# First filter products beside the last projections, and half of an output tile under the last inverse transforms

## The reference, cut to what matters

```python
parts = jnp.split(dwconv_centred(hy, hy_conv_w, hy_conv_b), 1 + HY_ORDER, axis=-1)
filters = hyena_filters(L, hy_w1, hy_b1, hy_w2, hy_b2, hy_w3, hy_freq)
u = parts[0]
for o in range(HY_ORDER):
    u = parts[o + 1] * long_conv(u, filters[:, o], hy_bias[o])
return jnp.concatenate([y, u], axis=-1) @ w_out, final

def long_conv(u, h, bias):          # y = irfft(rfft(u) * rfft(h)) + u * bias
```

## Time and profile before

| | before |
|---|---|
| median of 3 runs | 1463.18 us (1462.31 to 1465.86) |
| the profiled execution, own time | 1463.94 us |
| its span (first to last instruction) | 1462.1 us |
| TensorE busy | 1230.1 us, 84% of the span |
| last Hyena projection ends | 422.5 us |
| spectrum of turn 0 ends, turn 1's tokens begin | 448.8 us |
| turns 1 and 2, each | 26.9 us |
| output projection begins | 549.6 us |
| first expert slot free | 672.75 us |

### The profile page before, as it was taken

The page is one execution under the profiler, slowest core; times in us unless marked ns, Lnnn a source line. Parts: engine busy times, 40 slices in busy tenths (PEclk is TensorE's granted clock), DMA queues, the critical chain, the costliest instruction groups (busy, mean ns, idle before and its releaser), DMA issues.

```text
span 1462.1 us, 16614 instructions
## 1 busy us (share of the span) xinstructions
PE 1230.1 (84%) x6357; PEld 694.8 (48%) x6357; DVE 458.2 (31%) x950; ACT 338.1 (23%) x850; POOL 197.0 (13%) x267
## 2 busy tenths in 40 slices
PE   3899889899989989977997774699888959987771
PEld 1465454555445554455554442453455446544430
DVE  0104467533227860051111111321364341110104
ACT  3212276210022300041111111313253221111103
POOL 1000012100022301001211111125001011111101
PEclk9999999999999999988999998699999979999996
DMA  9985400276930125246999995933312559999993
GB/s 329 366 305 183 173 29 1 96 264 253 340 109 0 58 115 197 115 173 247 378 418 420 419 418 226 347 70 42 130 59 88 182 177 378 417 419 420 420 374 139
DMA packets 94494, 339.77 MB, mean 232 GB/s; under 512 B 12768, under 2 KB 16550, under 8 KB 69729
## 3 DMA queue, kind: packets, MB, share of 16 engines
q1 hardware_dynamic: 71296, 296.89, 52.0%
q0 software_dynamic: 16240, 35.08, 8.0%
q10 hardware_dynamic: 6897, 6.97, 1.4%
HBM read 336.69 MB, written 23.18 MB: 246 GB/s over the span
## 4 chain that ended last, share of the span: by engine, by line
PE 57%; DMA 18%; DVE 6%; ACT 3%; issue 2%; POOL 1%; ACTq 0%; DVEq 0%; POOLq 0%; SPq 0%
PE bank L780 52%; DMA ring<-in_moe_w_down_dram 17%; PE bank L784 4%; PE bank L811 1%; DMA arena<-expert_rows 1%; DVE arena L2247 1%; DVE arena L2249 1%; ACT ring L1768 0%; DMA hT<-rows,scr 0%; DVE xR L2251 0%; DMA expert_rows<-arena,scr 0%; POOL arena L2397 0%; ACT hT L1444 0%; ACT rstd L1418 0%; DVE arena L2269 0%
## 5 line engine op out<-in xcount | busy, mean ns | idle before, releaser
L780 PE MATMUL bank<-ring,arena 128*64 128x256 f32 (+4 forms) x2976 | 482.6, 434 | 64.4 <-DMA ring<-in_moe_w_down_dram 23.5
L780 PEld LDWEIGHTS bank<-ring,arena 128*64 128x64 f32 (+1 forms) x2976 | 247.2, 145 | 261.7 <-issue 147.2
L780 PE MATMUL bank<-hT,ring 128*128 128x384 f32 (+2 forms) x904 | 304.5, 498 | 6.4 <-ACT hT L1444 6.4
L780 PEld LDWEIGHTS bank<-hT,ring 128*128 128x128 f32 (+1 forms) x904 | 174.0, 194 | 134.6 <-issue 16.6
L2222 DVE TENSOR_TENSOR hT<-hT,bank 128x256 f32<-128x256 f32 x32 | 13.5, 421 | 279.4 <-ACT hT L1656 279.4
L780 PE MATMUL bank<-arena 128*64 128x32 bf16 (+9 forms) x560 | 76.5, 356 | 12.8 <-DVE arena L2195 4.5
L784 PE MATMUL bank<-cst,arena 128*128 128x128 f32 (+3 forms) x207 | 36.2, 335 | 60.7 <-ACT arena L1431 37.3
L780 PE MATMUL bank<-arena,ring 128*128 128x256 f32 (+3 forms) x272 | 63.1, 385 | 12.1 <-DVE ring L2083 7.0
L1656 ACT ACTIVATE hT<-bank 128x256 f32<-128x256 f32 x32 | 12.3, 384 | 260.9 <-PE bank L780 260.9
L784 PE MATMUL bank<-cst,hT 128*128 128x128 f32 x368 | 61.1, 301 | 12.2 <-DMA hT<-rows,scr 12.2
L784 PEld LDWEIGHTS bank<-cst,hT 128*128 128x128 f32 x368 | 47.4, 190 | 48.9 <-issue 35.9
(11 more groups left out here) (287 smaller groups left out, 1152.4 us busy)
## 6 DMA issues: line engine op xcount, KB each, us to landing
ring<-in_moe_w_gate_dram SPq DMA_DIRECT2D x30, 2048.0 KB, 19.6
ring<-in_moe_w_up_dram SPq DMA_DIRECT2D x30, 2048.0 KB, 21.5
ring<-in_moe_w_down_dram SPq DMA_DIRECT2D x30, 2048.0 KB, 22.4
ring<-in_w_ada_dram SPq DMA_DIRECT2D x24, 2048.0 KB, 14.7
ring<-in_ev_w_in_dram SPq DMA_DIRECT2D x11, 2048.0 KB, 11.5
ring<-in_ev_w_out_dram SPq DMA_DIRECT2D x4, 2048.0 KB, 15.1
arena<-expert_rows POOLq DMA_DIRECT2D x6, 1024.0 KB, 7.0
ring<-in_od_w_in_dram SPq DMA_DIRECT2D x3, 2048.0 KB, 21.0
```

The lines of the kernel that those rows point to most:

```text
L780: return nc.tensor.matmul(out, lhsT, rhs, start=start, stop=stop_, skip_group_check=True)
```

## The change

1. Turn 0's six filter products are issued right behind projection ("hy", 2, 5), with their copies on ScalarE and multiplications on GpSimd; they go to storage of their own (`pq0`, in `scr`, `rstdw` and the arena from 14336, where `gstage` lies), so ScalarE waits first until the gates are stored. `hs` is made on VectorE behind ("hy", 2, 3). The loads "hypar1" move to the slot of block ("ada", 1, 10) and so come right behind "hypar0"; the scratch slot becomes that of ("hy", 2, 1).
2. Turn 0's mirror product is issued behind the two H products.
3. The output projection's chunks 0 to 7 of token tile 0 (16 products) are issued in the last turn between spectrum and prompt inverse. The other tiles' chunks 0 to 7 follow the sample inverse without waiting for the gating; only from block 2 on is the gating waited for. The projection's banks are renumbered (`OUT_BANK`), also for the jobs behind it. `wout` 3 is loaded as soon as the last prompt inverse is done, behind one expert block in SP's list.

```diff
-HY_SLOTS = [k % NSLOT for k in (len(FIRST) - 6, len(FIRST) - 5)]
-HY_LENT = (len(FIRST) - 1) % NSLOT
+HY_PARAMS = [len(FIRST) - 6, len(FIRST) - 7]
+HY_SLOTS = [k % NSLOT for k in HY_PARAMS]
+HY_LENT = (len(FIRST) - 5) % NSLOT
+OUT_BANK = (6, 0, 1, 4, 5, 2, 3, 7)
+FILTERS_AFTER = ("hy", 2, 5)
...
         def own(*banks):
-            return banks if l == 0 else (None, None)
+            return tuple(OUT_BANK[b] for b in banks) if l == 0 else (None, None)
...
+        pq0 = ([scr[:, 0:512], rstdw[:, :]], area(14336, 2, 2, 512))
...
                 if k == len(FIRST) - 1:
-                    sp.wait_ge(done, JOB[LAST_INV] + 1)
+                    sp.wait_ge(done, JOB[LAST_SPEC_S] + 1)
...
+            def first_states():
+                pe.wait_ge(S("yn"), KD)
+                arrived(("wout", 0))
+                arrived(("wout", 1))
+                for h in range(2):
+                    took(pe, *PLAN[PRIOR[JOB[("wout", 0, h)]]][0])
+                    for k in range(KD):
+                        product(0, h, k)
+
+            def filters(turn, b, o):
+                for i, (s, x, t) in enumerate(HY_FILTERS):
+                    ps = open_bank("PQ", b, o, s, x, t)
+                    mm(ps[:, :], (hsP, hsQ)[x][:, cols(s + t)], w3s[:, b, o, :], True, True).then_inc(done, 1)
+                    if i == 0 and turn:
+                        mirror(b, o)
...
+                    if ("hy", q, c) == FILTERS_AFTER:
+                        pe.wait_ge(S("hs"), 1)
+                        pe.wait_ge(S("hypar0_in"), 16 * 6)
+                        filters(0, *HYO[0])
...
-            pe.wait_ge(S("hs"), 1)
             pe.wait_ge(S("hconv"), 3 * KD)
-            pe.wait_ge(S("hypar0_in"), 16 * 6)
...
-            filters(*HYO[0])
+            tokens(*HYO[0])
             prompt_response(0, *HYO[0])
+            mirror(*HYO[0])
             sample_response(0, *HYO[0])
             for turn, (b, o) in enumerate(HYO):
                 more = turn + 1 < len(HYO)
                 spectrum(b, o)
                 if more:
-                    filters(*HYO[turn + 1])
+                    tokens(*HYO[turn + 1])
+                    filters(turn + 1, *HYO[turn + 1])
+                else:
+                    first_states()
                 prompt_back(turn, b, o)
...
-            took(pe, *LAST_INV)
-            pe.wait_ge(S("yn"), KD)
...
                 for b in range(3):
                     arrived(("wout", b))
-                    for t in range(NT):
+                    if b == 2:
+                        took(pe, *LAST_INV)
+                    for t in range(1 if b < 2 else 0, NT):
...
+                if ("hy", c // KD, c % KD) == FILTERS_AFTER:
+                    act.wait_ge(S("gates_out"), 16 * 2)
+                    take_filters(0, *HYO[0])
...
-            for which, (block, b) in enumerate(((LOADS[len(FIRST) - 6], 0), (LOADS[len(FIRST) - 5], 1))):
+            for which, (block, b) in enumerate(((LOADS[HY_PARAMS[0]], 0), (LOADS[HY_PARAMS[1]], 1))):
```

More of the change, by code:

```diff
@@ L168, in bank_plan, with tokens, filters @@
                 job(("gr", 1), "act")
-    def filters(b, o):
+    def tokens(b, o):
         for t, bank in ((0, 6), (2, 7), (1, 6)):
             job(("utk", b, o, t), "act", None, bank)
+    def filters(b, o):
         for i, (s, x, t) in enumerate(HY_FILTERS):
             job(("PQ", b, o, s, x, t), "act", None, (7, 6, 1)[i % 3])
-            if i == 0:
+            if i == 0 and (b, o) != HYO[0]:
                 job(("rev", b, o), "dve", None, 0)
-    filters(*HYO[0])
     for turn in range(-1, len(HYO)):
@@ L190, in bank_plan @@
             job(("H", *HYO[turn + 1], 1), "act", None, 1)
+            if turn < 0:
+                job(("rev", *HYO[0]), "dve", None, 0)
         if turn >= 0:
@@ L973, in _ @@
             sum_squares("ssd", sqssd, KD)
[L976 to L995, removed]
-                                last = tr(ps[0:KD, cols(i)], mod[:, l, 16 + 24 * g:24 + 24 * g, v])
-                            last.then_inc(done, 1)
@@ L998, in _, with product @@
-            pe.wait_ge(S("hs"), 1)
-            pe.wait_ge(S("hconv"), 3 * KD)
-            pe.wait_ge(S("hypar0_in"), 16 * 6)
-            def tokens(b, o, t):
-                src = u0T if o == 0 else p1T
-                ps = open_bank("utk", b, o, t)
-                for c in range(4):
-                    last = tr(ps[:, cols(c)], src[:, b * 4 + c, cols(t)])
-                last.then_inc(done, 1)
-            def filters(b, o):
+            def product(t, h, k):
+                act_at = szT[:, k, cols(t)] if k < KD else hyT[:, k - KD, cols(t)]
+                return mm(banks[OUT_BANK[2 * t + h]], act_at, block_view(("wout", k // 4))[:, k % 4, wide(h)], k == 0, k == 2 * KD - 1)
@@ L1012, in filters, with mirror @@
                 for t in (0, 2, 1):
-                    tokens(b, o, t)
+                    ps = open_bank("utk", b, o, t)
+                    for c in range(4):
+                        last = tr(ps[:, cols(c)], src[:, b * 4 + c, cols(t)])
+                    last.then_inc(done, 1)
+            def mirror(b, o):
+                ps = open_bank("rev", b, o)
+                took(pe, "utk", b, o, 2)
+                mm(ps[:, :], flip, ut[:, 2, :], True, True).then_inc(done, 1)
+            def filters(turn, b, o):
                 for i, (s, x, t) in enumerate(HY_FILTERS):
@@ L1025, in prompt_response @@
                     ps = open_bank("H", b, o, x)
[L1026 removed]
+                    mm(ps[:, :], dft0[:, x, :], filt(turn, 0, x, 0), True, True).then_inc(done, 1)
             def sample_response(turn, b, o):
@@ L1568, in _, with take_filters @@
             root("ssd", D)
+            def take_filters(turn, b, o):
+                for s, x, t in HY_FILTERS:
+                    full(act, "PQ", b, o, s, x, t)
+                    A_(filt(turn, s, x, t), bank("PQ", b, o, s, x, t)[:, :], ACT.Copy).then_inc(taken["act"], 1)
             act.wait_ge(S("const"), 2)
@@ L1600, in _ @@
                     A_(ut[:, t, :], bank("utk", b, o, t)[:, :], ACT.Copy).then_inc(taken["act"], 1)
-                for s, x, t in HY_FILTERS:
-                    full(act, "PQ", b, o, s, x, t)
-                    A_(pq[s][:, x, t, :], bank("PQ", b, o, s, x, t)[:, :], ACT.Copy).then_inc(taken["act"], 1)
+                if turn:
+                    take_filters(turn, b, o)
                 full(act, "H", b, o, 1)
```

74 lines of the change are left out of this document (49 added, 25 removed).

## The result

| | before | changed |
|---|---|---|
| median, first comparison | 1463.84 us (1462.31 to 1465.86, 4 runs) | 1448.33 us (1446.81 to 1449.84, 4 runs) |
| the profiled execution, own time | 1463.94 us | 1446.81 us |
| its span | 1462.1 us | 1445.0 us |
| granted clock, mean | 0.945 | 0.951 |

The ratio is 0.9896 (95% interval 0.9882 to 0.991), 15.2 us of 1463.84. The profile after is of the fastest of the first four runs. The forecast was 1449.1 us, 14.1 us faster.

A forecast was written before the change was run, and what follows sets the result against it. TensorE's chain, then a saturated expert-weight stream whose start TensorE releases, was taken to bound the kernel. Gains of 3.5 and 11.1 less 0.5 make 14.1 us: forecast 1449.1 us, range 1446.0 to 1454.0.

The forecast's parts named there:

- hidden anyway: Rival: the expert-weight stream keeps its end whatever comes before, so gain 0, 1463.2 us; chance 0.03.
- Part 2: Last turn: 16 output-projection products between spectrum and prompt inverse remove idle time and low clock, 11.1 us, bounds 10.5 to 11.6.
- about 3: Last turn: low clock's share of the 11.08 us, about 3 us, beside 7.76 us idle; sample inverse 9.95 instead of 7.13.
- only half of the gain: Rival: gating or a bank holds TensorE behind the last sample inverse, half clock loses some 5 us: 1454 us; chance 0.04.
- Part 3: Renumbered banks: third tile's second half of token transposes waits for bank 6, costing 0.5 us, between 0 and 0.6.
- Part 1: Front: turn 0's filter products moved beside the projections, so turn 1's tokens start earlier: 3.5 us, range 2.5 to 4.5.
- Tokens at 430.32: Front: turn 0's token transposes start at 430.32, 0.06 us for the semaphore behind VectorE's last convolution at 430.26.
- Wait (b): ScalarE waits for the gates' store before the filter copies; free if landed by 414.0; counted 0, range 0 to 1 us.
- Wait (a): TensorE waits for "hypar0" behind ("hy", 2, 5); in time by about 1 us; counted 0, at most 1 or 2.
- 2.7 us decides nothing: Front: the remaining 2.7 us idle may or may not drop TensorE's clock, so the middle, 3.5 us, was taken.
- low-clock end of the range: Front at half clock until 5.6 us behind first transpose: takes 1.0 and first products 1.0 later; gain 2.7, bound 2.5 us.
- The slower rival: Gates' store lands late under added traffic, deciding from 428.1; landing at 435.8 gives 7.7 us slower, 1470.9 us; chance 0.05.

The follow-up runs named there:

- e5: The changed kernel again with no edit, profiled beside later runs: 1449.78 us; its clock fell to 0.50 about turn 0's tokens.
- e1: The kernel before with only the 16 output-projection products moved into the last turn, late gating wait and renumbered banks; filters unmoved: 1453.67 us, ratio 0.9921.
- e4: The kernel before with seven added products, results unread, between the last turn's prompt and sample inverses: 1460.48 us, ratio 0.9978.
- e2: The changed kernel with moved filters kept, but the output projection whole behind the last gating and banks in old order: 1459.96 us, ratio 0.9976.
- e3: The changed kernel with 8 instead of 16 output-projection products in the last turn, the other 8 behind the inverses: 1451.64 us, ratio 0.9914.
- e8: The changed kernel with filters behind ("hy", 2, 7) and the third tile's second half of normalised transposes in another bank: 1446.26 us, ratio 0.9875.
- e6: The changed kernel with the six filter products behind the last projection ("hy", 2, 7) instead of ("hy", 2, 5): 1447.06 us, ratio 0.9882.
- e7: The changed kernel with the filter products one projection earlier, behind ("hy", 2, 4) and the gates' transposes: 1456.43 us, ratio 0.9947.

## Why the prediction was right

**The coverage of the gain.** Rows 1 to 3 were read as: the expert stream is saturated, but TensorE releases its start. That held: the slot came 14.30 us earlier (658.45; forecast 658.7), 18 loads kept this, and the end followed. The chain still waits 26.96 us for a w_down block (27.20 in the earlier trace rows). The rival "hidden anyway" is refuted. The 658.7 was met because the clock held on the way: in e5 the slot came at 663.28.

**Part 2, forecast 11.1 us, measured 11.23.** No idle time and clock 1.00 from the spectrum to the projection, as forecast; e1 repeats it. The split into idle time and clock is confirmed by e4 for the kernel before (2.8 of the "about 3"); in e2 the clock's share was 1.9. The rival "only half of the gain" did not come; e3 shows how far it was: even half of the products would have kept the clock.

**Part 3, forecast -0.5 us, measured -0.46,** through the transposes named (first trace), and gone with the bank (e8). The prediction gave the clock no term on this tile. It cost 2.8 us there in e5, and some in e1, e2 and e3; e2 has the old banks and no pause between the transposes, so the new banks are not shown to be its cause.

**Part 1, forecast 3.5 us of 2.5 to 4.5.** Its steps one by one:
- Tokens at 430.32: measured 430.35. Spectrum's end 444.2 at the full clock: 444.43. First spectral product on VectorE 441.2: 441.30, by the time-ordered view.
- Wait (b), the gates' store, counted 0: it landed at 413.8. The 414.0 from which it was to cost assumed products from 412.0; they began at 411.86, and so the bound was 413.8 too. They took 5.35 us from start to start, in e6, where nothing waited for the store, 5.24: it cost 0.1 (0.2 in e5, 5.45). That it was near the bound at all is new with the change: see the last section.
- Wait (a), margin "about 1 us": e7 puts the landing 0.1 us ahead of the need. No cost here, but the margin was overstated, and not through the "hypar1" loads behind. The first decay block, the last of "hypar0", took 9.0, 10.2 and 9.1 us from issue to landing in the profiles without them (before, e1, e4) and 8.9 to 9.6 in the seven with them. Before, it was issued at 402.31 and so landed at 411.3, some tenths behind the last packets at 410 to 411. Over the ten profiles it landed 5.3 to 6.5 us behind the start of the gates' transposes, and it is wanted at 6.05: with a landing as late as e1's (6.5 us) the changed kernel would wait some 0.5 us, an estimate.
- "2.7 us decides nothing": shown by the two profiles of one kernel (e5). The Trainium skill, "TensorE: Matmul & The Clock Gate", Part 1 (the HAM clock gate), has a free-running window behind this. The traces agree in that behind the same 2.66 us pause the clock held in three profiles (the first, e2, e3) and fell in e5; no run here shows the window itself.
- The low-clock end of the range was mis-sized. I gave 1.0 us for the takes (ScalarE's copies that empty the banks) and 1.0 for the first products. From the first transpose to the G products e5 needs 437.58 - 429.31 = 8.27 us, the first profile 435.85 - 430.35 = 5.50: 2.8 us, of which 0.45 are the takes and the rest products, since the low level lasted to about 437.3 (0.50 in 436 to 437, 0.86 in 437 to 438, by the sums by stretch), 8 us behind the first transpose and not 5.6. Set beside the profile before, the bounds should have been 1.4 and 4.2; beside e1, whose old front took 45.80 us, they are 4.3 and 7.2. The forecast held the old front fixed. The 3.5 of e2's times lies between 1.4 and 4.2, but only one of its 12 runs has a profile, and an interval of 1.6 to 5.4 does not tell how often the clock fell in either kernel.

**The sum.** 4.4 + 11.2 - 0.5 = 15.2 us in the first pair of profiles, of which the first expert product's clock took 1.1 and the last pair's gave 1.7: clock again, in stages that the change leaves alone. The medians say 15.5 and 13.9, the forecast 14.1. That the last figure is so close is in part luck. The gain was 17.1 us by the first profile and 12.0 by e5's, with the same instructions; the clock decided 1.7 to 2.9 us at each of three places (the front, the third tile, the last expert pair), of which the forecast priced one, at the middle of its outcomes.

**The slower rival** (the store landing 14 us late) did not come: the store landed at 413.8, 14 us before the 428.1 from which it would have decided. The place was right, ScalarE did wait 1.22 us there. e7 shows what such a wait costs when it is exposed, for the loads and not for the store: the need comes one projection, 5.2 us, earlier, and nearly all of it turns into waiting.

## What to carry to other kernels

Look first for the engine's pauses on the path, not for work that could be done earlier: 7 discarded products in a pause made this kernel faster, and the best place for the filter products was the pause itself and not the place before it (e6 against the changed kernel, 2.95 us). Fill a pause up to the point where the wait ends and the clock holds; more brings little (0.62 us for the second eight products, in one trace each). When work moves ahead of loads or stores, take the landing from the consumer's wait and not from the queue's last packets, and follow each renumbered bank to the job that inherits it.

## What was not expected of the hardware

- One and the same pause of 2.66 us lowered TensorE's clock in the profiles of e5 and e7 and not in those of the changed kernel's first run, e2 and e3 (H products of 2.05 us and 1.10 us behind it). At 2.9 us it is a fifth of the whole gain, decided from run to run.
- The last expert pair's 16 records, 3.65 or 5.35 us behind the same pause of 2.35, move the second layer by 1.7 us in just the same way. Behind pauses of 2.0 to 2.6 us they took 5.35 in seven of the ten profiles and 3.65 in three (the changed kernel's two and e7). With the third tile, where the clock fell in e1, e2, e3 and e5, two single profiles of one kernel differ by 5.1 us with no work changed, and a step's size is better read between two points close to it than from the spans.
- The gates' store of two times 16 KB, issued from 407.59, landed at 413.8, 6.2 us later. Its packets (queue q10) moved in 411 to 414, beside loads that fill the engines. In 410 to 411 us the DMA queues show one row for the changed kernel (queue: packets, MB, share of 16 engines), where the earlier trace rows have two:

```profile
q0 software_dynamic: 106, 0.39, 104.2%
```

In the kernel before, issued at 407.75, 78 of its 80 packets moved in 409 to 411, 42 of them in the earlier trace rows. What differs in that stretch is the "hypar1" loads, which now follow "hypar0" in q0. All ten profiles go that way: without them (before, e1, e4) the store's first packet moves 1.6 to 2.0 us behind its issue, with them (the seven others, e2 with part 1 alone among them) 3.6 to 3.8 us. So the added loads delayed a store in another queue by nearly 2 us and took up the margin of wait (b). The prediction had added traffic at this place in its slower rival, and nothing for it in its sum.
